# One-core block of mixers and experts on Trainium2: the work ahead of the first projection dealt out anew over VectorE, ScalarE and GpSimd

## The reference

```python
def rmsnorm(x, g):
    x32 = x.astype(jnp.float32)
    y = x32 * lax.rsqrt(jnp.mean(x32 * x32, axis=-1, keepdims=True) + EPS)
    return (y * g.astype(jnp.float32)).astype(x.dtype)

h = rmsnorm(x, norm1_g[l])
u = h @ w_in[l]
...
x = x + jnp.concatenate([y_a, y_b, y_c], axis=-1) @ w_out[l]
h = rmsnorm(x, norm2_g[l])
x = x + hierarchical_moe(h, ...)
...
return rmsnorm(x, final_g)
```

## Time and profile before

| | us |
|---|---|
| runs, median of 3 (lowest to highest) | 1321.22 (1320.35 to 1321.64) |
| the profiled execution, its own time | 1320.74 |
| span of its trace, first to last instruction | 1318.9 |
| TensorE busy | 1235.8 (94%) |
| VectorE busy | 556.1 (42%) |
| ScalarE busy | 286.3 (22%) |
| GpSimd busy | 6.0 (0%) |
| first product of the projection begins at | 14.19 |

### The profile page before, as it was taken

The page is one execution under the profiler, slowest core; times in us unless marked ns, Lnnn a source line. Parts: engine busy times, 40 slices in busy tenths (PEclk is TensorE's granted clock), DMA queues, the critical chain, the costliest instruction groups (busy, mean ns, idle before and its releaser), DMA issues.

```text
span 1318.9 us, 15728 instructions
## 1 busy us (share of the span) xinstructions
PE 1235.8 (94%) x5942; PEld 648.2 (49%) x5942; DVE 556.1 (42%) x982; ACT 286.3 (22%) x400; POOL 6.0 (0%) x27
## 2 busy tenths in 40 slices
PE   8999999999999999999898899989998999898995
PEld 7888888888874333333333333333333333333332
DVE  5576988775565323232322223223222222332234
ACT  6443454474441111101001000010100001101003
POOL 1000000000000000000000000000000000000000
PEclk9999999999999999999999999999999999999998
DMA  8655454457489999999999999999999999999995
GB/s 310 213 186 179 147 192 162 158 176 303 159 335 341 433 430 432 428 432 431 432 430 432 431 432 430 432 431 432 430 432 431 432 430 432 431 432 430 428 428 242
DMA packets 65473, 471.76 MB, mean 358 GB/s; under 512 B 6135, under 2 KB 6647, under 8 KB 38428
## 3 DMA queue, kind: packets, MB, share of 16 engines
q1 hardware_dynamic: 65436, 471.24, 87.0%
HBM read 469.13 MB, written 2.10 MB: 357 GB/s over the span
## 4 chain that ended last, share of the span: by engine, by line
PE 60%; DMA 33%; DVE 3%; issue 2%; ACT 1%; DVEq 0%; SPq 0%; ACTq 0%
DMA ring<-in_w_up 22%; PE bank L1783 20%; DMA zone_u<-in_w_up 10%; PE bank L1542 10%; PE bank L1550 8%; PE bank L1819 8%; PE bank L1832 5%; PE bank L1551 4%; PE bank L1753 1%; PE bank L1784 1%; DVE zone_u L1000 1%; PE bank L1553 1%; DMA x_tok<-in_x 1%; ACT gatesT L845 1%; PE bank L1794 0%
## 5 line engine op out<-in xcount | busy, mean ns | idle before, releaser
L1783 PE MATMUL bank<-ring,win 128*64 128x512 f32 x816 | 377.3, 617 | 42.2 <-DMA ring<-in_w_up 29.8
L1784 PE MATMUL bank<-ring,win 128*64 128x512 f32 x832 | 378.6, 608 | 0.0
L1783 PEld LDWEIGHTS bank<-ring,win 128*64 128x64 f32 x816 | 112.0, 141 | 285.4 <-issue 265.1
L1550 PE MATMUL bank<-h_both,w_hi 128*128 128x512 f32 x540 | 192.5, 399 | 0.7 <-DVE h_both L939 0.4
L1371 DVE SCALAR_TENSOR_TENSOR x_tok<-bank,gate_of,x_tok 128x512 f32<-128x512 f32 x256 | 174.4, 744 | 24.8 <-PE bank L1832 23.8
L1819 PE MATMUL bank<-ring,hiddenT 128*64 128x512 f32 x688 | 154.4, 594 | 11.3 <-ACT gatesT L845 11.3
L395 DVE TENSOR_TENSOR w_lo<-stage,w_hi 128x2048 fp32r<-128x2048 f32 x59 | 134.6, 2287 | 63.7 <-ACT w_hi L389 63.6
L1551 PE MATMUL bank<-h_both,w_lo 128*128 128x256 f32 x540 | 151.5, 280 | 0.0
L837 ACT ACTIVATE rows_now<-bank,root_row 64x512 f32<-64x512 f32 x32 | 21.8, 680 | 550.5 <-PE bank L1784 550.5
L389 ACT ACTIVATE w_hi<-stage 128x2048 fp32r<-128x2048 f32 x59 | 113.4, 1922 | 125.6 <-PE bank L1551 82.0
L1832 PE MATMUL bank<-y_rows,gatesT 64*128 64x512 f32 x512 | 126.9, 615 | 1.0 <-DVE y_rows L1395 1.0
(11 more groups left out here) (251 smaller groups left out, 1026.9 us busy)
## 6 DMA issues: line engine op xcount, KB each, us to landing
ring<-in_w_up SPq DMA_DIRECT2D x49, 2048.0 KB, 31.6
ring<-in_w_gate SPq DMA_DIRECT2D x47, 2048.0 KB, 34.8
ring<-in_w_down SPq DMA_DIRECT2D x41, 2048.0 KB, 31.6
stage<-in_w_in SPq DMA_DIRECT2D x43, 1024.0 KB, 5.0
zone_u<-in_w_down SPq DMA_DIRECT2D x19, 2048.0 KB, 31.7
zone_u<-in_w_up SPq DMA_DIRECT2D x9, 2048.0 KB, 33.6
zone_u<-in_w_gate SPq DMA_DIRECT2D x9, 2048.0 KB, 35.0
stage<-in_w_out SPq DMA_DIRECT2D x16, 1024.0 KB, 4.9
```

The lines of the kernel that those rows point to most:

```text
L1550: M.matmul(dst[:, :], hi[:, at], both, start=(c == 0), stop=False)
L1783: M.matmul(dst[0:W_ROWS, :], rows_of[:, c, 0:W_ROWS], gate[:, at], start=(c == 0), stop=(c == C - 1))
L1784: ins = M.matmul(dst[UPPER, :], rows_of[:, c, 0:W_ROWS], up[:, at], start=(c == 0), stop=(c == C - 1))
```

## The change

It moves and cuts work in the first 25 us of the program only.

- The square of tile 1's last 512 features goes from ScalarE to VectorE, which adds three partial sums in place of two.
- Of tile 0 VectorE scales chunks 0 to 7 only; of tile 1 chunks 0 to 3 as before. GpSimd scales chunks 8 to 15 of tile 0 (as soon as `rstd_made` is 1), then chunks 4 to 7 and 8 to 15 of tile 1. ScalarE scales none.
- Chunks 0 to 3 are turned into other halves: chunks 0 and 2 into the two halves of bank 4, chunks 1 and 3 into those of bank 5 (`turned_in`). ScalarE takes chunk 0 once all four are turned, and VectorE waits for single chunks of them, not pairs.
- TensorE turns chunks 4 to 7 of tile 1 after the pairs of chunk 1, not before the first product.
- The second weight chunk is split in two halves of 1024 columns (`second_hi`, `second_lo`), each followed by two chunks of x.

```diff
+        def turned_in(c):
+            at, half = (4 + c % 2, c // 2) if c < CM else (4 + c // 2 % 4, c % 2)
+            return bank[at][:, half * S:(half + 1) * S]
...
             link(pool.memset(rw[:, :, GROUPS:GW], 0.0))
+
+            def scaled_rest(t, cs):
+                return pool.tensor_scalar(h_tok_c[:, t, cs, :], x_tok_c[:, t, cs, :], RSTD[:, t:t + 1], None, ALU.mult)
+
+            pool.wait_ge(rstd_made, 1)
+            scaled_rest(0, slice(2 * CM, C)).then_inc(h_rest, 1)
+            pool.wait_ge(rstd_made, 2)
+            scaled_rest(1, slice(CM, 2 * CM)).then_inc(h_quarter[1], 1)
+            scaled_rest(1, slice(2 * CM, C)).then_inc(h_rest, 1)
...
-                    at = slice(h * HD, (h + 1) * HD)
+                    at = slice(h * HD, D - NB if t and h else (h + 1) * HD)
...
-                    act.wait_ge(turned, k + 1)
-                    for i in range(2):
-                        nc.scalar.activation(hT_hi[:, 2 * k + i, :], bank[4 + k % 4][:, i * S:(i + 1) * S], ACT.Copy,
-                                             scale=g1[:, 2 * k + i:2 * k + i + 1]).then_inc(turned_act, 1)
+                    act.wait_ge(turned, max(k + 1, 2))
+                    for c in (2 * k, 2 * k + 1):
+                        if k == 1:
+                            act.wait_ge(turned_dve, c - 1)
+                        nc.scalar.activation(hT_hi[:, c, :], turned_in(c), ACT.Copy, scale=g1[:, c:c + 1]).then_inc(turned_act, 1)
...
-            act.wait_ge(rstd_made, 1)
-            nc.scalar.activation(h_tok_c[:, T - 1, CM:2 * CM, :], x_tok_c[:, T - 1, CM:2 * CM, :], ACT.Copy,
-                                 scale=RSTD[:, T - 1:T]).then_inc(h_quarter[1], 1)
...
-            split_hi(act, 0, 0, 1)
-            turned_hi(range(2, 4))
+            act.wait_ge(w_loaded[1], 16)
+            for h in range(2):
+                at = slice(h * 2 * NB, (h + 1) * 2 * NB)
+                nc.scalar.activation(w_hi[1][:, at], stage[1][:, at], ACT.Copy).then_inc(hi_made if h else second_hi, 1)
+                turned_hi(range(2 + h, 3 + h))
...
-                    dve.wait_ge(turned_act, 2 * (c // 2) + 2)
+                    dve.wait_ge(turned_act, c + 1 if c < CM else 2 * (c // 2) + 2)
...
+            scaled(0, slice(0, 2 * CM)).then_inc(h_ready, 1)
+            dve.wait_ge(x_loaded[1][1], 16)
+            V.scalar_tensor_tensor(h_tok[:, 1, D - NB:], x_tok[:, 1, D - NB:], 1.0, x_tok[:, 1, D - NB:], ALU.mult, ALU.mult,
+                                   accum_out=sq_parts[:, 1, 2:3]).then_inc(sum_sq, 1)
+            dve.wait_ge(sum_sq, 5)
+            link(V.tensor_reduce(SS[:, 1:2], sq_parts[:, 1, 0:3], AX.X, ALU.add))
...
-            scaled(slice(2 * CM, C)).then_inc(h_ready, 1)
-            split_lo(dve, 0, 0, 1)
-            turned_lo(range(CM, 2 * CM))
+            for h in range(2):
+                at = slice(h * 2 * NB, (h + 1) * 2 * NB)
+                if h:
+                    dve.wait_ge(hi_made, 2)
+                else:
+                    dve.wait_ge(second_hi, 1)
+                V.tensor_tensor(w_lo[1][:, at], stage[1][:, at], w_hi[1][:, at].bitcast(F32),
+                                ALU.subtract).then_inc(lo_made if h else second_lo, 1)
+                turned_lo(range(CM + 2 * h, CM + 2 * h + 2))
...
                     if k >= 4:
-                        pe.wait_ge(turned_dve, 2 * (k - 3))
+                        pe.wait_ge(turned_dve, max(2 * (k - 3), CM))
...
             turn(range(2), T - 1)
-            pe.wait_ge(h_quarter[1], 1)
-            turn(range(2, 4), T - 1)
             keep(KEEP_SPLIT)
...
                 if m == 1:
-                    pe.wait_ge(h_ready, T)
+                    pe.wait_ge(h_rest, 2)
...
+                    elif m == 1 and i < 2:
+                        pe.wait_ge(second_lo, 1)
...
                         ins = channel_pair(bank[j], w_hi[m % PARTS], w_lo[m % PARTS], c, i, j)
+                    if c == 1:
+                        pe.wait_ge(h_quarter[1], 1)
+                        turn(range(2, 4), T - 1)
```

More of the change, by code:

```diff
@@ L218, in hybrid_moe_program @@
         rstd_made = sem("rstd_made")
+        second_hi = sem("second_hi")
+        second_lo = sem("second_lo")
+        h_rest = sem("h_rest")
         h_quarter = [sem(f"h_quarter{q}") for q in range(2)]
@@ L914, in _, with scaled @@
             dve.sem_inc(att_copied, HALF_HEADS)
-            for t in range(T):
-                dve.wait_ge(sum_sq, 2 * t + 2)
-                link(V.tensor_tensor(SS[:, t:t + 1], sq_parts[:, t, 0:1], sq_parts[:, t, 1:2], ALU.add))
-                V.tensor_scalar(MS[:, t:t + 1], SS[:, t:t + 1], 1.0 / D, EPS, ALU.mult, ALU.add).then_inc(mean_sq, 1)
-                dve.wait_ge(root, t + 1)
-                if t == 0:
-                    link(V.reciprocal(RSTD[:, t:t + 1], RT_[:, t:t + 1]))
-                    V.tensor_scalar(h_tok[:, t, :], x_tok[:, t, :], RSTD[:, t:t + 1], None, ALU.mult).then_inc(h_ready, 1)
-            def scaled(cs):
-                return V.tensor_scalar(h_tok_c[:, T - 1, cs, :], x_tok_c[:, T - 1, cs, :], RSTD[:, T - 1:T], None, ALU.mult)
+            dve.wait_ge(sum_sq, 2)
+            link(V.tensor_tensor(SS[:, 0:1], sq_parts[:, 0, 0:1], sq_parts[:, 0, 1:2], ALU.add))
+            V.tensor_scalar(MS[:, 0:1], SS[:, 0:1], 1.0 / D, EPS, ALU.mult, ALU.add).then_inc(mean_sq, 1)
+            dve.wait_ge(root, 1)
+            V.reciprocal(RSTD[:, 0:1], RT_[:, 0:1]).then_inc(rstd_made, 1)
+            dve.wait_ge(rstd_made, 1)
+            def scaled(t, cs):
+                return V.tensor_scalar(h_tok_c[:, t, cs, :], x_tok_c[:, t, cs, :], RSTD[:, t:t + 1], None, ALU.mult)
             def first_chunk_lo(c):
@@ L936, in turned_lo @@
                 for c in cs:
-                    dve.wait_ge(turned_act, 2 * (c // 2) + 2)
-                    at = (c % 2) * S
-                    V.scalar_tensor_tensor(hT_lo[:, c, :], bank[4 + c // 2 % 4][:, at:at + S], g1[:, c:c + 1],
+                    dve.wait_ge(turned_act, c + 1 if c < CM else 2 * (c // 2) + 2)
+                    V.scalar_tensor_tensor(hT_lo[:, c, :], turned_in(c), g1[:, c:c + 1],
                                            hT_hi[:, c, :].bitcast(F32), ALU.mult, ALU.subtract).then_inc(turned_dve, 1)
-            V.reciprocal(RSTD[:, T - 1:T], RT_[:, T - 1:T]).then_inc(rstd_made, 1)
-            dve.wait_ge(rstd_made, 1)
-            scaled(slice(0, CM)).then_inc(h_quarter[0], 1)
+            scaled(0, slice(0, 2 * CM)).then_inc(h_ready, 1)
[4 more added lines that the diff above has]
+            link(V.tensor_reduce(SS[:, 1:2], sq_parts[:, 1, 0:3], AX.X, ALU.add))
+            V.tensor_scalar(MS[:, 1:2], SS[:, 1:2], 1.0 / D, EPS, ALU.mult, ALU.add).then_inc(mean_sq, 1)
+            dve.wait_ge(root, 2)
+            V.reciprocal(RSTD[:, 1:2], RT_[:, 1:2]).then_inc(rstd_made, 1)
+            dve.wait_ge(rstd_made, 2)
+            scaled(1, slice(0, CM)).then_inc(h_quarter[0], 1)
             first_chunk_lo(0)
@@ L1506, in turn @@
                     if k >= 4:
-                        pe.wait_ge(turned_dve, 2 * (k - 3))
-                    for i in range(2):
-                        ins = M.transpose(bank[4 + k % 4][:, i * S + t * P:i * S + (t + 1) * P],
-                                          h_tok_c[:, t, 2 * k + i, :], ident[:, :])
+                        pe.wait_ge(turned_dve, max(2 * (k - 3), CM))
+                    for c in (2 * k, 2 * k + 1):
+                        ins = M.transpose(turned_in(c)[:, t * P:(t + 1) * P], h_tok_c[:, t, c, :], ident[:, :])
                     if t == T - 1:
```

2 lines of the change are left out of this document (1 added, 1 removed).

## The result

The changed kernel took 1323.82 us in the median of 22 executions (1321.63 to 1325.44), the kernel before, beside it on the same chip, 1320.79 us (22 executions, 1320.27 to 1322.60): a ratio of 1.0019 with a 95% interval of 1.0013 to 1.0025. The forecast was 1320.7 us, no change that can be told, with a range of 1319.0 to 1322.3; the measured median is 1.5 us above its upper end, and the interval shows a small but real loss. The profiled execution of the changed kernel took 1324.07 us, its span is 1322.3 us, 3.4 more than before.

What follows compares the result with a forecast made beforehand. Projections were taken as bound by TensorE, experts by weight DMAs. First product -0.65, moved transposes +0.53 and banks -0.41 sum to -0.53 us; from 1321.22 that gives 1320.7 us, no change that can be told, range 1319.0 to 1322.3.

Steps and rivals of the forecast that it cites:

- Loads follow PE, so a shift at the beginning reaches the end: Whole kernel: DMA loads wait for TensorE's progress, not the clock, so time gained ahead of 22.35 us moves everything behind it.
- the one on GpSimd: Beginning: GpSimd's three scalings end by 14.0 us, ahead of TensorE's need, and cost zero.
- Its price: GpSimd's scalings: 2.05 ns an element, from a two-input operation of 512; 1.6 ns was the other end.
- the one priced: Ahead of m = 1: GpSimd's last scaling comes late and TensorE waits; 1324 us, chance 0.05.
- So no slowing: GpSimd beside VectorE: VectorE's operations took 0.40 us with GpSimd running and 0.41 without, all reading one PSUM input.
- rival 1: Beginning: GpSimd and VectorE slow each other, operations taking twice as long; net +0.6 us, 1321.8 us, chance 0.22.
- the won 0.65: First product: comes at 13.54 us, not 14.19, which is 0.65 us sooner.
- The prediction's last sentence: Measured median: the prediction calls itself wrong if it lies outside 1318.6 to 1323.9 us.
- the second root: Ahead of tile 1's transposes: the shorter ScalarE square ends 0.45 us sooner, so transposes start at 11.57 us.
- The term for the banks, -0.41: Transposes ahead of m = 1: no wait for emptied banks is left, 2.53 us become 2.12, 0.41 us won.
- that cover of 0.4 us: Banks ahead of m = 1: 0.4 us in hand; without it TensorE waits for bank 7 as before.
- 0.53: Transposes moved among the pairs: four add 0.53 us of TensorE's time, a pure cost.

Runs made afterwards that it cites:

- experiment 2: Kernel before plus three GpSimd scalings into a buffer nobody reads, no other part of the change: 1324.01 us, ratio 1.0022.
- experiment 5: Changed kernel with GpSimd's scalings walking the same elements in runs of 8 neighbours (or 4): 1320.57 us, ratio 1.0000; the profiled execution took 1324.31 us.
- experiment 8: Changed kernel, unchanged, executed twice more for profiles: 1324.96 and 1322.54 us.
- experiment 6: Changed kernel, GpSimd's scalings held until VectorE scaled its tile 1 part: 1325.89 us; second kernel, GpSimd scaling only tile 1's chunks 8 to 15: 1320.76 us.
- experiment 3: Changed kernel with the whole square back on ScalarE, GpSimd's scalings kept: 1324.46 us, ratio 1.0025.
- experiment 1: Changed kernel with GpSimd's scalings taken out and done by VectorE: 1321.15 us, ratio 0.9999.
- second kernel of experiment 7: Changed kernel with GpSimd walking runs of 8 and more small TensorE products (28 and 16, not 8 and 6): 1320.60 us, ratio 0.9999.

## Why the prediction was wrong

**Loads follow PE, so a shift at the beginning reaches the end: right.** 3.9 us at 26.5 us became 3.3 at the milepost and 3.4 at the end, only with the other sign. Of the other profiles two have over 0.6 us more at the end than at the milepost, that of experiment 2 (1.1 us) and that of experiment 5 (2.8 us), so a single execution can carry that much from elsewhere.

**The step that failed is the one on GpSimd**, its price and its overlap with VectorE, in three places.

1. *Its price.* I took 2.05 ns an element from an operation of 512 with two inputs, and named 1.6 and 2.05 as the ends. Alone it is 4.8 ns by chunks and 3.0 in a row. A row of another operation, with another step, was no bound. The consequence was not the one priced, though: PE asked for the last scaling at 19.6 by the forecast and in the profiled execution after 24 us, so `h_rest` never showed; it did at 0.83 and at 3.0 us in experiments 8 and 6.
2. *The overlap: "So no slowing".* The row at 25.18 ran beside operations that read PSUM, and those are not held in the changed kernel either (0.88 for two). The text said so, and then rival 1 went by "twice as long" for the square alone. It took 3.4 times its time (+1.66 us). What is held is not slowed by a factor: the longest holds added 1.77 us to a scaling of 1.29 us, 1.76 and 1.71 to scalings of 0.69, and 1.6 to a subtraction of 1.22.
3. *The scaling of tile 1*, on the path to the first product, was in no term. It was held for 1.0 us in the changed kernel, for 1.7 us in experiment 3. 1.66 and 1.0 less the won 0.65 are 2.0 of the 2.3 us at the first product; the rest is the transposes and small products at the lower clock (1.12 us for four, not 0.72).

Rival 1 (0.22) had the right pair of engines, a slowing by a factor in place of a hold, and about a third of the price: it added 0.69 + 0.4 = 1.1 us to a forecast of -0.5, where 3.5 were needed for the 3.0 us measured. The prediction's last sentence, wrong only outside 1318.6 to 1323.9, is wider than its range; the result lies inside it by 0.1 us and well outside the range. The lost clock was in no rival; it comes on top in some executions, 1.3 and 1.4 us in the two pairs of profiles above.

The Trainium skill has a rule that I had not weighed: SBUF — State Buffer, section "Who interferes with whom", says that the pair of ports which VectorE and GpSimd share is an exclusive lock, and of VectorE's two-port modes that the one that issues first has it for the whole instruction while the other blocks. The two profiles of experiment 8 agree that order decides (2.29 against 0.68 us for the same square). On "the whole instruction" the measurements differ. The scaling of 512 ended 0.5 us behind GpSimd's first operation in the changed kernel and in experiments 2 and 3. All the others held behind an operation of 1024 by chunks were through well before it ended: the square at 11.50 with GpSimd at work until 13.55, the subtraction at 20.30 (21.93), the scalings of experiment 2 at 11.01 and 20.55 (13.01 and 22.63) and of experiment 6 at 14.46 (16.70). Taken less their own time they were let in 2.7 to 3.3 us before GpSimd's end, that is about the middle of its operation; why there, no run shows.

The same section says that a VectorE instruction with at most one SBUF input, outside its two-port modes, does not contend; the scaling of 512 with a step of 16 takes 0.69 us, over twice the time per element of the 2048 in a row (1.29 us), and was clearly held in seven profiles (1.41 to 2.45 us). Whether it ran in a two-port mode no run here shows. The line of the Trainium skill that the prediction drew on, GPSIMD Engine Reference, section "8. Key points", names the two-port modes beside the two SBUF inputs; the prediction left that half out, and the scalings with it. The same page, section "4.1 Engine selection", has one-input operations at roughly line rate; 3.0 ns an element in a row is far from VectorE's 0.63.

**Without GpSimd the forecast of the beginning was nearly right, in part by errors that cancel.** Experiment 1 had the second root and the first product where the prediction put them: transposes of tile 1 at 11.51 (11.57), first product at 13.55 (13.54). The term for the banks, -0.41, rests on the 1.18 us that GpSimd takes off VectorE; with VectorE doing it a wait of 0.41 us for bank 7 stayed, as the prediction said ("If that cover of 0.4 us is gone, PE waits for bank 7 as before"). Without that term (-0.65 + 0.53) the forecast is -0.1 us, and +0.1 was measured, within what can be told. Two prices in the sum were misread: 0.53 us is how long four weight loads take from the first's start to the last's end, not what four transposes add. The four among the pairs added 0.37 us (16.45 to 16.82 in experiment 1), and sixteen without a wait took 1.73 us, not 2.12 (20.77 to 22.50 in the second kernel of experiment 7), so with no wait left this stretch wins 0.80 us, not 0.41. Against that the sixteen pairs of m = 0 took 5.8 us in experiment 1, where the forecast had 5.6.

**The best version.** Runs of 8 with more small products had the best median against the kernel before, 0.46 us less. The interval of its ratio (0.9990 to 1.0009) holds 1, so nothing here beats the kernel before by a difference that can be told.

## What to carry to other kernels

Before you give an idle GpSimd a piece of VectorE's work, look at what VectorE does in the meantime, not only at whether GpSimd is done in time: here 5 us of GpSimd held the operation that the critical path waited for. Price such an operation by one of its own kind and step, run alone, and not by the nearest row. A hold hangs on the other's operation and not on one's own: it added up to 1.8 us to operations of 0.69 us and of 1.29 us alike, behind GpSimd operations of about 5 us, so "twice as slow" is no bound for a short operation. And before a long time is put down to the beginning, look at a milepost in the middle: here one execution of 1324.31 us lost most of it behind 602 us.
